# Routing, end and input of a four-layer fp32 model on one core, with 20 token slots as pairs of four k tiles by 512 columns

## The chip, the cores and the metric

One core of a Trainium2 chip (trn2). PE is TensorE (matmul), PEld its weight load, DVE VectorE, ACT ScalarE, POOL GpSimd, SP SyncE, which here only issues DMAs. All times are device microseconds of one execution of the whole program; the metric is the median of several executions, lower is better.

## The reference

Input x is 1 x 256 x 1024, all in float32. Two blocks of two layers each follow one another. Cut to what matters:

```python
# first block: an even layer, an odd layer, then rms_norm(x, final_norm)
def even_layer(x, g_norm, w_in, b_f, w_out):
    z = rms_norm(x, g_norm) @ w_in          # 8208 columns: qa ka va ga fa qb kb vb gb
    ya = forgetting_attention(qa, ka, va, log_sigmoid(fa + b_f))   # 16 heads of 64
    yb = dilated_attention(qb, kb, vb)                             # 16 heads of 64
    return x + concat([ya * silu(ga), yb * silu(gb)]) @ w_out
def odd_layer(x, g_norm, w_in, w_out):
    q, k, v, g = split(rms_norm(x, g_norm) @ w_in)     # 1024, 1024, 2048, 2048 columns
    y = head_group_norm(retention(rotate(q), rotate(k) / 16, v))   # 4 heads, v of 512
    return x + (y * silu(g)) @ w_out
# second block: layer_norm, then twice
    h = layer_norm(ALPHA * h + hybrid_mixer(h, ...))   # sparse attention and a short convolution
    h = layer_norm(ALPHA * h + f)                      # f: swiglu (l = 0), then
def moe_swiglu(h, w_router, wg, wu, wd):               # f of l = 1: 8 experts, 2 of them per token
    top_v, top_i = top_k(h @ w_router, 2)
    gate = sum(one_hot(top_i) * softmax(top_v))
    return sum(gate[e] * (silu(h @ wg[e]) * (h @ wu[e])) @ wd[e] for e in range(8))
```

## The kernel before

The 256 tokens are two tiles (NT, t = 0, 1) of 128; the model width is eight k tiles (KD). Weights come as **slots** of 128 x 2048 float32 (1 MB), 275 in all. For each slot SP issues a load into a raw buffer (L437; two raw buffers before the experts, four in them), ACT copies it rounded to fp32r into `w_hi` (`split_hi`, L1197), DVE writes the remainder to `w_lo` (`split_lo`, L1520), and PE multiplies each pair of operands in three matmuls: high with high, high with low, low with high (`parts_mm`, L566 to L568). The activations are split the same way (`x_hi`, `x_lo`; `y_hi`, `y_lo`; `t_hi`, `t_lo` at the routing). `w_hi`/`w_lo` are rings of four before the experts and three in them; `ahead(s)` on ACT and DVE splits slot s + 4 (or s + 3) once slot s is through. Each engine's instructions run in the order written; semaphores order them across engines: `lo_done` (slot ready), `used` (slot multiplied), `g_free` (one of three result banks `g_ps` free), `n_h`, `n_tr`, `n_hi`, `n_lo` (halves of a norm's rows, transposes and splits).

A **token slot** (`token_slot`) holds all eight k tiles for 256 output columns: per token tile eight k steps, each with a 128 x 128 block of x as the stationary operand and 256 weight columns moving, 48 matmuls in all. `rows_slot` has the weights stationary and 256 tokens moving, also 48. Output slots (`out_slot`) and expert slots have four k tiles and 512 columns, and so 24 and 12 matmuls of 512.

Order of the work. *Start:* norm 0 of both token tiles with `begin(0, ...)`: x is normalized on DVE (`summed`, `ready`, `finish`; POOL computes the inverse root as a power, `root`, DVE refines it, `newton`), transposed by PE, split, and multiplied with slots 0 and 1 as it comes. Slots 0 to 3 are the first v; then `narrow_product` (16 columns: forget gates) and slots 4 to 11. *Even layer:* two attentions of eight pairs of heads; PE runs one slot in each step (`among`): slots 12 to 23 and the gates 24 to 31, the second v being 20 to 23. *Retention:* v slots 40 to 47, q and k 48 to 55, gates 56 to 63. In the head loop PE does scores of head h, a gate slot (`G_AFTER`), and the head's output once DVE has the decayed scores (`decayed`, L1928, semaphore `r_dec`) and the norm of the head before (`r_norm`, L1954). ACT applies Silu to the gate slot, DVE multiplies (`gate_slot`, L1936, `r_y`). *Routing* (after slot 142, norm 5): per token tile the product with the router (`narrow_part`, 8 columns, 24 matmuls); the top two (`router`, L1701 to L1733, small DVE operations, each after the last); the ranks by two small matmuls; one-hot selections (`select`, L1743); `gather` (32 matmuls, L571) makes the transposed rows of the first two experts. `keep_busy` issues matmuls that nobody reads. The number of rounds is computed at L1731 to L1733, and `m_loops` releases it: SP waits for it before the load of slot 147 (`sp.wait_ge(m_loops, 1)`). *Experts:* four rounds of 33 slots, two experts each: `gate_up` (22), `down` (11), results scattered back by matmuls (`scatter`) at the end. *End:* the last scatter, two sums per token tile (L2182, L1567), norm 6 and two output DMAs (L462).

## Time and profile before

| | |
|---|---|
| median of 3 runs | 1439.88 us (1438.84 to 1441.04) |
| profiled execution | 1441.42 us, span 1439.6 us |
| PE, DVE, ACT, POOL busy | 96%, 68%, 53%, 7% |
| DMA | 305.84 MB, 212 GB/s over the span |
| chain that ended last | PE 75%, DVE 11%, DMA 4%, issue 4%, ACT 4% |

The span is the time from the first to the last instruction. Busy shares are averages over stages with different limits; the chain is followed back from the last instruction, so its shares tell which engine the end depended on. A matmul's recorded duration overlaps the next one's: the pace is the distance between starts.

### The profile page before, as it was taken

The page shows a single profiled execution, that of the slowest core. Times are in us where ns is not written, and L with a number is a line of the kernel's source. Part 1 is how long each engine was busy: PE and PEld are TensorE (multiplying, and loading weights), DVE is VectorE, ACT ScalarE, POOL GpSimd, SP SyncE. Part 2 cuts the span into 40 slices and gives each one's busy share as a digit, 9 for nine tenths or more (in the row PEclk, how much of TensorE's full clock was granted, in tenths as well). Part 3 has the DMA queues.
Part 4 walks back from the last instruction along what each step waited for, and adds up shares of the span by engine and source line. Part 5 has one row for each costly group of instructions (what it writes and reads, how often), then busy time and mean ns, then how long its engine had stood idle before and what let it go on. Part 6 is the DMA issues. An engine that isn't in the chain of part 4 may idle for free.

```text
span 1439.6 us, 22664 instructions
## 1 busy us (share of the span) xinstructions
PE 1384.1 (96%) x9117; PEld 1229.2 (85%) x9117; DVE 978.5 (68%) x1354; ACT 759.1 (53%) x915; POOL 101.6 (7%) x112
## 2 busy tenths in 40 slices
PE   5999999999999999999999999999999999999995
PEld 5999998789988889888999889887888888888883
DVE  5445656564766476867544476858788898898887
ACT  3445468425333327743443336742677677677672
POOL 1000013100001210001222010002000000000000
PEclk9999999999999999999999999998999999999998
DMA  6543344436543635534555545540798988889985
GB/s 223 194 178 143 118 147 146 145 135 232 192 147 118 219 126 189 192 106 164 203 188 190 180 154 201 195 163 31 299 355 315 342 326 341 344 323 356 327 334 218
DMA packets 43674, 305.84 MB, mean 212 GB/s; under 512 B 4864, under 2 KB 5120, under 8 KB 7744
## 3 DMA queue, kind: packets, MB, share of 16 engines
q1 hardware_dynamic: 41328, 295.69, 55.7%
q0 software_dynamic: 2256, 8.88, 1.8%
q8 instruction: 64, 1.05, 0.3%
q14 instruction: 26, 0.21, 0.0%
HBM read 303.51 MB, written 1.05 MB: 212 GB/s over the span
## 4 chain that ended last, share of the span: by engine, by line
PE 75%; DVE 11%; DMA 4%; issue 4%; ACT 4%; POOL 1%; DVEq 0%; SPq 0%; POOLq 0%; ACTq 0%
PE g_ps L566 18%; PE g_ps L568 17%; PE g_ps L567 17%; PE a_ps L566 4%; DMA raw<-w_dram 4%; PE a_ps L568 4%; PE a_ps L567 4%; PE a_ps L571 4%; DVE w_lo L1520 3%; ACT w_hi L1197 3%; PE a_ps L575 2%; PE o_ps L571 2%; DVE tiny L1567 1%; DVE x L1651 1%; POOL tiny L481 1%
## 5 line engine op out<-in xcount | busy, mean ns | idle before, releaser
L1520 DVE TENSOR_TENSOR w_lo<-raw,w_hi 128x2048 fp32r<-128x2048 f32 x240 | 548.6, 2291 | 233.3 <-ACT w_hi L1197 230.5
L1197 ACT ACTIVATE w_hi<-raw 128x2048 fp32r<-128x2048 f32 x240 | 459.7, 1915 | 245.4 <-PE a_ps L568 91.1
L566 PE MATMUL g_ps<-w_hi,x_hi 128*128 128x256 f32 (+1 forms) x720 | 244.8, 340 | 12.5 <-DVE x_lo L1617 8.5
L566 PE MATMUL g_ps<-x_hi,w_hi 128*128 128x256 f32 x880 | 252.6, 287 | 0.0
L567 PE MATMUL g_ps<-x_lo,w_hi 128*128 128x256 f32 x880 | 249.9, 284 | 0.0
L568 PE MATMUL g_ps<-x_hi,w_lo 128*128 128x256 f32 x880 | 249.8, 284 | 0.0
L568 PE MATMUL g_ps<-w_hi,x_lo 128*128 128x256 f32 (+1 forms) x720 | 239.3, 332 | 0.0
L567 PE MATMUL g_ps<-w_lo,x_hi 128*128 128x256 f32 (+1 forms) x720 | 239.0, 332 | 0.0
L566 PEld LDWEIGHTS g_ps<-x_hi,w_hi 128*128 128x128 f32 x880 | 169.8, 193 | 4.0 <-issue 3.9
L567 PEld LDWEIGHTS g_ps<-x_lo,w_hi 128*128 128x128 f32 x880 | 169.8, 193 | 0.0
L568 PEld LDWEIGHTS g_ps<-x_hi,w_lo 128*128 128x128 f32 x880 | 169.7, 193 | 0.0
L566 PEld LDWEIGHTS g_ps<-w_hi,x_hi 128*128 128x128 f32 x720 | 137.8, 191 | 29.4 <-DVE w_lo L1520 10.6
L566 PE MATMUL a_ps<-w_hi,y_hi 128*128 128x512 f32 x384 | 151.8, 395 | 3.9 <-DVE w_lo L1520 1.9
L568 PE MATMUL a_ps<-w_hi,y_lo 128*128 128x512 f32 x384 | 149.8, 390 | 0.0
L567 PE MATMUL a_ps<-w_lo,y_hi 128*128 128x512 f32 x384 | 149.7, 390 | 0.0
L568 PEld LDWEIGHTS g_ps<-w_hi,x_lo 128*128 128x128 f32 x720 | 137.8, 191 | 13.1
L567 PEld LDWEIGHTS g_ps<-w_lo,x_hi 128*128 128x128 f32 x720 | 138.1, 192 | 12.2 <-issue 0.2
L1520 DVE TENSOR_TENSOR w_in_raw<-raw,w_in_raw 128x2048 fp32r<-128x2048 f32 x35 | 80.2, 2291 | 54.9 <-ACT w_in_raw L1197 54.9
L566 PEld LDWEIGHTS a_ps<-w_hi,y_hi 128*128 128x128 f32 x384 | 72.1, 188 | 20.6 <-issue 4.5
L568 PEld LDWEIGHTS a_ps<-w_hi,y_lo 128*128 128x128 f32 x384 | 72.1, 188 | 15.4
L1197 ACT ACTIVATE w_in_raw<-raw 128x2048 fp32r<-128x2048 f32 x35 | 66.9, 1911 | 33.6 <-DMA raw<-w_dram 15.1
L567 PEld LDWEIGHTS a_ps<-w_lo,y_hi 128*128 128x128 f32 x384 | 72.2, 188 | 14.0
(287 smaller groups left out, 1996.7 us busy)
## 6 DMA issues: line engine op xcount, KB each, us to landing
raw<-w_dram SPq DMA_DIRECT2D x279, 1024.0 KB, 4.9
arena<-rows_dram POOLq DMA_DIRECT2D x3, 1024.0 KB, 5.4
x<-x_dram SPq DMA_DIRECT2D x2, 512.0 KB, 6.8
extra<-extra_dram POOLq DMA_DIRECT2D x1, 1024.0 KB, 5.6
extra<-rows_dram POOLq DMA_DIRECT2D x2, 512.0 KB, 3.7
y_spare<-rows_dram POOLq DMA_DIRECT2D x4, 256.0 KB, 4.8
out_dram<-x SPq DMA_DIRECT2D x2, 512.0 KB, 2.7
extra<-gains_dram SPq DMA_DIRECT2D x1, 512.0 KB, 4.5
```

The lines of the kernel that those rows point to most:

```text
L481: pool.tensor_tensor(tiny[:, 228 + t0:228 + t0 + n], tiny[:, 224 + t0:224 + t0 + n], tiny[:, 226 + t0:226 + t0 + n], ALU.pow).then_inc(roo ...
L566: pe.matmul(ps, lh, rh, start=start, stop=False, skip_group_check=True)
L567: pe.matmul(ps, lh, rl, start=False, stop=False, skip_group_check=True)
L568: return pe.matmul(ps, ll, rh, start=False, stop=stop, skip_group_check=True)
L571: return pe.matmul(ps, lhs, rhs, start=start, stop=stop, skip_group_check=True)
L575: return pe.transpose(ps, src, ident)
L1197: act.activation(w_hi[w_place(s)][:, :], raw[PLACE[s]][:, :], ACT.Copy).then_inc(hi_done, 1)
L1520: dve.tensor_tensor(w_lo[w_place(s)][:, :], raw[PLACE[s]][:, :], w_hi[w_place(s)][:, :].bitcast(F32), ALU.subtract).then_inc(lo_done, 1)
L1567: own(dve.bn_stats(tiny[:, 200 + 12 * t + 6 * b:206 + 12 * t + 6 * b], xs))
L1651: own(dve.scalar_tensor_tensor(xs, xs, scale, out_bank(t, b)[:, :], ALU.mult, ALU.add))
```

## The change

The layout of the weights, their number and bytes stay as they are; 20 slots hold other elements.

- **Input.** The host passes x also transposed, `xT`, and the first norm's gain as eight columns. Slots 0 to 3 are multiplied with the unnormalized `xT` times gain, split into `y_hi`, `y_lo` (`plain_slot`), and the copies of their results are scaled by the token's inverse root. PE starts with nine matmuls that nobody reads. The inverse roots are broadcast by two transposes, DVE scales `xT` from that bank, and one split makes `x_hi`, `x_lo` for slot 4 on. Order and queue position of the first DMAs change; `small` and `extra` are issued later by POOL.
- **Wide slots.** The second even v (20 to 23), retention's v (40 to 47) and gates (56 to 63) become pairs: a slot holds four k tiles and 512 columns, its pair the other four; two result banks (one per token tile) stay open over both, and are copied after the second. The decay of head h + 1 moves ahead of the moments of head h.
- **Routing.** The router product is made like the second block's gates: high and low part side by side as 48 stationary columns (`small_rows`), copied by ACT, added by `fold_rows`. POOL makes only the first `t_lo`, after norm 5, and DVE the second. The splits of slots 144 and 145, the counts (`round_counts`) and the memset of the accumulator move behind the selection. The fillers go from 16 + 14 + 4 to 3 + 12 + 8. Slot 143 needs only half of x_lo.
- **End.** The first expert's half of the last scatter goes ahead of the last two slots, which are multiplied by column halves. The sums come with the additions, the variance from ACT (Square with accumulation), and four output DMAs replace two.

The core of the diff (indentation cut by eight):

```diff
-    load_x(0)
-    sp.dma_start(extra[:, G_AT:G_AT + D], a["gains"][0]).then_inc(gain_in, 16)
-    sp.dma_start(const[:, 0:P], a["const"][:, 0:P]).then_inc(ident_in, 16)
+    sp.dma_start(const[:, 0:C_CAUSAL], a["const"][:, 0:C_CAUSAL]).then_inc(ident_in, 16)
+    for b in range(2):
+        sp.dma_start(xT[:, 4 * b:4 * b + 4, :], a["xT"][:, 4 * b:4 * b + 4, :]).then_inc(xT_in[b], 16)
     load(0, 0)
-    load_x(1)
     load(1, 1)
-    sp.dma_start(const[:, P:N_CONST], a["const"][:, P:N_CONST]).then_inc(const_in, 16)
+    for t in range(NT):
+        load_x(t)
+    sp.dma_start(const[:, C_CAUSAL:N_CONST], a["const"][:, C_CAUSAL:N_CONST]).then_inc(const_in, 16)
     sp.dma_start(vec[:, :], a["vec"]).then_inc(vec_in, 16)
     for s in range(2, MOE + PLACES):
         load(s, s)
...
+        for b in range(2):
+            cols = slice(512 * b, 512 * b + 512)
+            sp.wait_ge(n_h, 4 * 6 + 2 * t + b + 1)
+            sp.dma_start(out.rearrange("b (t p) d -> p (b t) d", p=P)[:, t, cols], x[:, t, cols]).then_inc(out_done, 16)
+    sp.wait_ge(out_done, 64)
...
+    pool.dma_start(small_raw, a["small"].rearrange("p k (a b) -> p k a b", a=3)).then_inc(small_in, 16)
     pool.wait_ge(n_h, 4)
-    pool.dma_start(extra[:, G_AT:G_AT + D], a["gains"][1]).then_inc(odd_gain_in, 16)
+    pool.dma_start(extra[:, 0:E_ALL], a["extra"][0][:, 0:E_ALL]).then_inc(extra_in, 16)
+    pool.wait_ge(n_lo, 4)
+    pool.dma_start(extra[:, G_AT:G_AT + D], a["gains"][0]).then_inc(odd_gain_in, 16)
...
             for t in range(NT):
-                pool.wait_ge(m_thi, t + 1)
-                pool.tensor_tensor(t_lo[:, t, :], x[:, t, :], t_hi[:, t, :].bitcast(F32),
-                                   ALU.subtract).then_inc(m_tlo, 1)
-            load_both_rows(6)
-            two_roots()
+                a_ = tiny[:, 224 + t:225 + t]
+                pool.wait_ge(e_var, t + 1)
+                own(pool.tensor_tensor(a_, end_var[:, t:t + 1], end_eps, ALU.add))
+                own.sync()
...
+    def wide_mm(s, half, t, ks):
+        w = weights(s + half, (4, 512))
+        for k in ks:
+            mm = parts_mm(g_ps[bank_of(s + t)][:, :], pick(from_x, lambda u: u[:, k, t * P:(t + 1) * P]),
+                          pick(w, lambda u: u[:, k - 4 * half, :]), k == 0, k == KD - 1)
+        return mm
...
+    def wide_slot(s, half):
+        pe.wait_ge(lo_done, s + half + 1)
+        for t in range(NT):
+            if half == 0:
+                wide_free(s, t)
+            mm = wide_mm(s, half, t, range(4 * half, 4 * half + 4))
+        mm.then_inc(used, 1)
...
+    def small_rows(i, seg):
...
         def part_of(t, ks):
             for k in ks:
                 parts_come(i, t, k)
                 to = slice(t * P, (t + 1) * P)
...
+                pe.matmul(a_ps[0][0:48, to], small[:, k, seg, :, :].rearrange("p a b -> p (a b)"), x_hi[:, k, to],
...
-                mm = pe.matmul(a_ps[0][0:24, to], small[:, k, 1 + l, 0, :], x_lo[:, k, to],
+                mm = pe.matmul(a_ps[0][0:24, to], small[:, k, seg, 0, :], x_lo[:, k, to],
...
+    def plain_slot(s):
+        w = weights(s, (KD, S))
+        if s > 0:
+            pe.wait_ge(lo_done, s + 1)
+        if g_nth[s] > 0:
+            pe.wait_ge(g_free[bank_of(s)], g_nth[s])
+        for half in range(2):
+            if s == 0 and half == 0:
+                pe.wait_ge(half_lo, 1)
+            elif s == 0:
+                pe.wait_ge(lo_done, 1)
+            for t in range(NT):
+                for k in range(4 * half, 4 * half + 4):
+                    if s == 0 and t == 0:
+                        pe.wait_ge(u_lo, k + 1)
+                    mm = parts_mm(g_ps[bank_of(s)][:, t * S:(t + 1) * S],
+                                  pick(from_y, lambda u: u[:, k, t * P:(t + 1) * P]),
+                                  pick(w, lambda u: u[:, k, :]), k == 0 and t == 0, k == KD - 1)
+        mm.then_inc(used, 1)
+    pe.wait_ge(u_hi, 4)
+    early = y_hi[:, 0:2, :].rearrange("p a b -> p (a b)")
+    for _ in range(9):
+        pe.matmul(g_ps[2][:, :], early[:, 0:P], early[:, :], start=True, stop=True, skip_group_check=True)
+    for s in range(2):
+        plain_slot(s)
     pe.wait_ge(ident_in, 16)
-    begin(0, token_part(0, 0), token_part(0, 1))
+    pe.wait_ge(n_h, 4)
+    for t in range(NT):
+        tr = turned(a_ps[0][:, t * P:(t + 1) * P], tiny[:, 228 + t:229 + t].to_broadcast([P, P]))
+    tr.then_inc(n_tr, 4)
     for s in range(2, 4):
-        even_slot(s)
+        plain_slot(s)
+    pe.wait_ge(n_lo, 4)
     pe.wait_ge(small_done, 1)
     narrow_product(0, HF)
...
-    keep_busy(16, 2, G_ALL)
+    keep_busy(3, 2, G_ALL)
+    fold_rows(DEPTH)
+    keep_busy(12, 2, G_ALL)
...
-    keep_busy(14, 2, G_ALL)
+    keep_busy(8, 2, G_ALL)
...
-    keep_busy(4, 2, G_ALL)
...
-        pe.wait_ge(m_xlo, 4 + 4 * i)
+        pe.wait_ge(m_xlo, (4 if earlier else 2) + 4 * i)
...
+                    pe.wait_ge(m_xlo, 4)
                 if u == 5:
...
+            return
+        pe.wait_ge(m_hid, UNITS + UNITS * i)
+        pe.wait_ge(m_osb, 2 + 4 * i)
+        for t in range(NT):
+            for n in range(2):
+                scatter(banks[t][n], t, n, 0, True, False)
+        for n in range(2):
+            for c in (UNITS - 2, UNITS - 1):
+                pe.wait_ge(lo_done, MOE + FT + c + 1 + 33 * i)
+                for k in range(2):
+                    mm = half_of(c, k, n)
+                if n == 1:
+                    mm.then_inc(used, 1)
+                elif c == UNITS - 1:
+                    mm.then_inc(m_first, 1)
...
+    act.wait_ge(ident_in, 16)
+    for k in range(KD):
+        act.wait_ge(xT_in[k // 4], 16)
+        act.activation(y_hi[:, k, :], xT[:, k, :], ACT.Copy, scale=norm_col[:, k:k + 1]).then_inc(u_hi, 1)
+    act.wait_ge(raw_in[0], 16)
+    act.activation(w_hi[0][:, 0:SLOT // 2], raw[0][:, 0:SLOT // 2], ACT.Copy).then_inc(half_hi, 1)
+    act.activation(w_hi[0][:, SLOT // 2:], raw[0][:, SLOT // 2:], ACT.Copy).then_inc(hi_done, 1)
+    for s in range(1, RING_BEFORE):
+        split_hi(s, 0, s)
+    act.wait_ge(n_h, 4)
+    even_slot(0)
+    for b in range(2):
+        act.wait_ge(zT_made, 4 * b + 4)
+        act.activation(x_hi[:, 4 * b:4 * b + 4, :], xT[:, 4 * b:4 * b + 4, :], ACT.Copy).then_inc(n_hi, 2)
+    act.wait_ge(small_in, 16)
+    act.activation(small_hi, small_raw, ACT.Copy).then_inc(small_hi_done, 1)
...
-        s = OD_G + u
-        act.wait_ge(used, s + 1)
-        if u >= 3:
-            act.wait_ge(r_y, u - 2)
-        act.activation(gate_view(s), g_ps[bank_of(s)][:, :], ACT.Silu).then_inc(g_free[bank_of(s)], 1)
-        ahead(s)
+        act.wait_ge(used, OD_G + u + 1)
+        for e in ((u - 1, u) if u % 2 else ()):
+            s = OD_G + e
+            if e >= 3:
+                act.wait_ge(r_y, e - 2)
+            act.activation(gate_view(s), g_ps[bank_of(s)][:, :], ACT.Silu).then_inc(g_free[bank_of(s)], 1)
+        ahead(OD_G + u)
...
-            ahead(L_WO[l] + 2 + t)
+            if not (l and t):
+                ahead(L_WO[l] + 2 + t)
             if l:
                 act.wait_ge(n_h, 4 * i + 2 * t + 2)
                 act.activation(t_hi[:, t, :], x[:, t, :], ACT.Copy).then_inc(m_thi, 1)
+        if l:
+            act.wait_ge(narrow_full, 2 + DEPTH)
+            act.activation(rows24, a_ps[0][0:48, 0:S], ACT.Copy).then_inc(rows_copied, 1)
+            ahead(L_WO[l] + 3)
...
+                if not last:
+                    act.wait_ge(used, MOE + FT + (6 if e == 0 else 11) + 33 * i)
                 act.wait_ge(m_back, 1 + i)
                 for n in range(2):
...
+                act.wait_ge(e_mean, t + 1)
+                act.activation(unread[:, t, :], x[:, t, :], ACT.Square, bias=end_bias[:, t:t + 1], scale=D ** -0.5,
+                               accum_out=end_var[:, t:t + 1]).then_inc(e_var, 1)
...
-        rest_of_norm(i, lambda: tile(0), lambda: tile(1), (last, last + 1))
+        rest_of_norm(i, lambda: tile(0), lambda: tile(1), () if i == 5 else (last, last + 1))
...
+        dve.wait_ge(rows_folded, 1 + DEPTH)
+        chain(lambda: dve.tensor_copy(lg, a_ps[1][:, 0:64].rearrange("p (a b) -> p a b", a=2)[:, :, HF:HF + NE]))
         best(on1, mx[0])
         chain(lambda: dve.scalar_tensor_tensor(lg, on1, NEG, lg, ALU.mult, ALU.add))
...
-    dve.wait_ge(gain_in, 16)
+    dve.wait_ge(ident_in, 16)
+    for k in range(KD):
+        dve.wait_ge(u_hi, k + 1)
+        dve.scalar_tensor_tensor(y_lo[:, k, :], xT[:, k, :], norm_col[:, k:k + 1], y_hi[:, k, :].bitcast(F32),
+                                 ALU.mult, ALU.subtract).then_inc(u_lo, 1)
+    halves = slice(0, SLOT // 2), slice(SLOT // 2, SLOT)
+    for half, made, done in zip(halves, (half_hi, hi_done), (half_lo, lo_done)):
+        dve.wait_ge(made, 1)
+        dve.tensor_tensor(w_lo[0][:, half], raw[0][:, half], w_hi[0][:, half].bitcast(F32), ALU.subtract).then_inc(done, 1)
+    split_lo(1, 0, 1)
     for t in range(NT):
         dve.wait_ge(x_in[t], 16)
         for b in range(2):
             summed(0, t, b)
         ready(0, t)
-        finish(0, t)
-        split_lo(t, 0, t)
-        low_part(0, t)
+    for t in range(NT):
+        dve.wait_ge(root_done, asked[t])
+        newton(tiny[:, 224 + t:225 + t], tiny[:, 228 + t:229 + t], tiny[:, 230 + t:231 + t])
+    dve.tensor_copy(tiny[:, 240:242], tiny[:, 228:230]).then_inc(n_h, 4)
+    split_lo(2, 0, 2)
+    dve.wait_ge(n_tr, 4)
+    for k in range(KD):
+        dve.scalar_tensor_tensor(xT[:, k, :], xT[:, k, :], norm_col[:, k:k + 1], a_ps[0][:, 0:S],
+                                 ALU.mult, ALU.mult).then_inc(zT_made, 1)
+    split_lo(3, 0, 3)
...
-        dst = rv[:, :, u * S:(u + 1) * S]
-        dve.tensor_tensor(dst, dst, gate_view(s).rearrange("p (a b) -> p a b", a=2), ALU.mult).then_inc(r_y, 1)
+        dst = rv[:, u % 2, u // 2 * RV:(u // 2 + 1) * RV]
+        dve.tensor_tensor(dst, dst, gate_view(s), ALU.mult).then_inc(r_y, 1)
...
     gated = 0
+    decayed(0)
     for h in range(RH):
-        decayed(h)
         for u in G_AFTER[h]:
             ahead(OD_G + u)
-            while gated <= u and gated < 2 * h:
+            while (gated | 1) <= u and gated < 2 * h:
                 gate_slot(gated)
                 gated += 1
+        if h < RH - 1:
+            decayed(h + 1)
         dve.wait_ge(r_out, h + 1)
...
+        ahead(L_WO[1] + 2)
...
+        ahead(L_WO[1] + 3)
+        round_counts()
+        dve.memset(f_acc[:, :, :], 0.0).then_inc(m_acc, 1)
...
+            own(dve.tensor_tensor_reduce(xs, xs, banks[t][n][:, :], 1.0, 0.0, ALU.add, ALU.add, end_sum[:, t, n:n + 1]))
+        def mean_of(t):
             own.sync()
-            summed(6, t, n)
-        dve.wait_ge(m_sct, 2 * before + 1)
+            dve.tensor_scalar(end_bias[:, t:t + 1], end_sum[:, t, 0:1], end_sum[:, t, 1:2], -D ** -1.5,
...
+        def scattered(n):
+            dve.wait_ge(m_sct, 2 * before + 1 + n)
+            own(dve.tensor_tensor(tiny[:, 238 + n:239 + n], const[:, 0:1], const[:, 1:2], ALU.add))
...
-        gathered(0, 1)
-        ready(6, 0)
-        centre(6, 0)
-        finish(6, 0)
...
+        scattered(1)
+        for t in range(NT):
+            gathered(t, 1)
+            mean_of(t)
+        for t in range(NT):
+            y = tiny[:, 228 + t:229 + t]
+            own.sync()
+            own(dve.scalar_tensor_tensor(z[:, t, :], x[:, t, :], end_mean[:, t:t + 1], gain_of(6), ALU.add, ALU.mult))
+            roots.append(0)
+            dve.wait_ge(root_done, len(roots))
+            newton(tiny[:, 224 + t:225 + t], y, tiny[:, 230 + t:231 + t])
+            for b in range(2):
+                dve.scalar_tensor_tensor(x[:, t, cols(b)], z[:, t, cols(b)], y, bias_of(6, b), ALU.mult, ALU.add).then_inc(n_h, 1)
...
+def wide_slots(w):
+    n = w.shape[1] // 512
+    return w.reshape(2, 4, P, n, 512).transpose(3, 0, 2, 1, 4).reshape(2 * n, P, SLOT)
```

## Rows read from the trace of the kernel before

**Rows 1.** page: busy time of each engine; granted clock in 40 slices

```profile
PE 1384.1 (96%) x9117; PEld 1229.2 (85%) x9117; DVE 978.5 (68%) x1354; ACT 759.1 (53%) x915; POOL 101.6 (7%) x112
...
PEclk9999999999999999999999999998999999999998
```

**Rows 2.** waits of PE: who waited for whom, total us, times, longest

```profile
PE a_ps L575 <- DVE arena L1604: 9.5, 1, 9.5
```

**Rows 3.** timeline of PE (start us, us): 256 columns, then 512

```profile
255.81 0.28 PE L567 MATMUL g_ps<-x_lo,w_in_raw 128*128 128x256 f32 x1
...
258.45 0.28 PE L568 MATMUL g_ps<-x_hi,w_in_raw 128*128 128x256 f32 x1
...
800.15 0.39 PE L566 MATMUL a_ps<-w_in_raw,y_hi 128*128 128x512 f32 x1
...
804.68 0.39 PE L568 MATMUL a_ps<-w_in_raw,y_lo 128*128 128x512 f32 x1
```

**Rows 4.** chain of waits to 32 us (start, us), then timeline rows

```profile
2.13 9.08 DMA raw<-w_dram
...
13.18 2.29 DVE w_lo L1520
...
45.77 0.17 PE L566 MATMUL a_ps<-small,x_hi 128*128 128x16 f32 x1
...
405.56 0.43 DVE L1919 TENSOR_TENSOR arena<-part 128x256 f32<-128x256 f32 x1
```

**Rows 5.** windows: busy us per engine, PEclk, DMA share, GB/s

```profile
23.00:25.60 2.60, 2.54 (x12) 2.54 (x12) 0.00 (x1) 0.00 (x0) 0.00 (x0) 0.50 0.81 265
...
409.90:477.30 67.40, 64.90 (x442) 56.90 (x442) 41.59 (x66) 22.12 (x22) 9.86 (x10) 1.00 0.37 132
993.10:998.40 5.30, 5.24 (x25) 5.24 (x25) 5.10 (x4) 2.88 (x3) 2.34 (x1) 0.50 0.00 0
```

**Rows 6.** chain of waits in retention, start and us

```profile
426.88 4.15 PE a_ps L571 x14
...
447.88 2.41 PE a_ps L571 x5
```

**Rows 7.** routing: DVE timeline, chain row, PE timeline

```profile
985.89 3.44 DVE L1594 SCALAR_TENSOR_TENSOR x<-x,tiny,extra 128x1024 f32<-128x1024 f32 x1
...
998.89 1.72 DVE L1702 TENSOR_TENSOR tiny<-tiny 128x16 f32<-128x16 f32 x1
...
1004.61 1.76 DVE L1723 MEMSET arena<- 128x2048 f32 x1 [0.38 <-issue]
...
1008.57 4.11 PE a_ps L571 x32
...
534.79 0.22 PE L706 MATMUL a_ps<-x_hi,small 128*48 128x128 f32 x1
...
535.69 0.22 PE L708 MATMUL a_ps<-x_lo,small 128*24 128x128 f32 x1
```

**Rows 8.** PE at slot 147, page's loads, chain, window of a round

```profile
1025.23 0.48 PE L566 MATMUL g_ps<-w_hi,x_hi 128*128 128x512 f32 x1
...
raw<-w_dram SPq DMA_DIRECT2D x279, 1024.0 KB, 4.9
...
1108.78 8.66 DMA raw<-w_dram
...
1084.10:1187.50 103.40, 102.67 (x503) 85.38 (x502) 90.09 (x73) 74.01 (x65) 0.00 (x0) 1.00 0.89 336
```

**Rows 9.** the end: chain row, DVE, POOL, and SP's output transfers

```profile
1420.17 1.40 PE g_ps L571 x6
...
1427.38 1.28 DVE L1594 SCALAR_TENSOR_TENSOR x<-x,tiny,arena 128x1024 f32<-128x1024 f32 x1
...
1427.56 1.53 POOL L481 TENSOR_TENSOR tiny<-tiny 128x1 f32<-128x1 f32 x1 [426.28 <-DVE tiny L1584]
...
1431.14 5.73 SPq L462 DMA_DIRECT2D out_dram<-x  x2
```

180 lines of the change are left out of this document (104 added, 76 removed).

## The prediction

> **What bounds the kernel now.** I read the page first. PE is busy 96% of the span and its granted clock is full in nearly every slice [rows 1], so a gain has to come from fewer PE columns or loads, from stretches where PE runs at the low clock, or from the gaps. The waits of PE itself are short in sum; the largest single one is the first transpose, 9.5 us [rows 2]. The steady stretches are paced by PE alone. In one, 22 intervals of a 256-column matmul take 2.64 us (0.120 us each, 48 to a slot: 5.76 us); in another, 20 intervals with 512 columns take 4.53 us (0.2265 us each, 24 to a slot: 5.44 us) [rows 3]. The chain of waits leaves PE in four places that this change touches: the first 28 us, the four heads of retention, the routing at 985 to 1014 us, and the end after 1420 us.
>
> **The start.** Today PE waits for the load issued at 2.13 that lands at 11.21, its split on ACT (1.92) and DVE (2.29), and the split of the normalized x; then, half-way, for a second norm and split. Slot 3 ends as the narrow product begins, at 45.77 us [rows 4]. It also works 23.0 to 25.6 us at half clock [rows 5].
> After the change no PE work before slot 4 needs the norm. The DMA order becomes constants (68 KB), transposed x (1 MB), slot 0, slot 1, x. That is 732 KB less ahead of slot 0 than today; 2,848 KB landed in the 9.08 us to 11.21, so its share is 2.3 us and slot 0 lands at about 8.9 (estimate). Half a slot on ACT is half of 1.92 plus latency, 1.05, and on DVE 1.2: PE starts at 11.25. The scaled splits of x (8 on ACT of about 0.35, 8 on DVE of about 0.43, the 128x256 row of [rows 4]) lie under the load of slot 0, and the nine warm-up matmuls (512 columns at half clock, twice 0.2265, 4.1 us from about 6.1) too. From there four slots of 5.76 and two small transposes (0.4) follow: 11.25 + 23.04 + 0.4 = 34.7.
> What could be late is checked by chaining the rows. Slot 1: lands 11.5, ACT to 13.4, DVE to 15.9, wanted at 17.0. DVE then does the sums of squares (4 of about 0.65), the two roots' newton steps (0.6 each) and posts the root at 20.4; slot 2's low part ends at 22.7 and PE wants it at 23.3. The eight scalings of the transposed x out of PSUM take 8 x 0.40 = 3.3, and slot 3's low part ends at 28.8, wanted at 29.0. The ACT queue has a new long wait: it scales slot 0's output and then stands on the load of slot 4 (issued at 22.7, landed 27.5) before it makes x_hi; behind it x_hi and x_lo end at 32.9 and the small weights at 34.2, just before PE asks. **Gain 45.8 - 34.7 = 11.1**, with 9 to 13 as ends: a cold first slot costs 1.3 (14 matmuls at 0.21 instead of 0.12 [rows 4, 5]), a scaling of 0.69 instead of 0.40 each costs 2.1, and and a first load as much earlier again as the estimate above says gives 2.
>
> **Wide slots.** 20 slots go from 5.76 to 5.44 us: 0.32 each. The four of the second v: 1.28, less 0.3 because both banks of the last pair are now copied (2 x 0.6 on ACT) before the scores may start: **1.0**. The eight v slots of retention run back to back, the copy of a pair needs banks that PE wants 2.7 us later: **2.6**. Of the eight gate slots four lie inside the head loop, where PE does not set the pace alone. There the chain goes from the end of a gate slot through Silu, ACT's split, DVE's split 2.29, moments, root, the two scalings, and decay, to the next outputs: from 416.95 to 426.88, and a similar one, with the gate products, ends at 447.88 [rows 6]. Moving the decay ahead of the moments shifts 0.55 us within that chain and saves nothing; two Silus before a split instead of one add 0.5 us to every second chain. By that arithmetic the loop ends 0.4 later after its first slot than now. Outside it two slots give 0.32 each ahead of the loop, slot 62 gives 0.32, and slot 63 with the wait for y_lo 1.15 (DVE has no gate product ahead of the casts there), less 0.3 for the last turned outputs, which wait for both last gate products. **1.4**, between 0.4 and 2.6.
>
> **Routing.** Four things leave the path. POOL's t_lo runs beside DVE's centring of x, which takes 3.44 us instead of 1.28: 2.15. The second t_lo holds a 16-column operation for 1.72 instead of 0.17: 1.55. The 24 narrow matmuls per token tile at half clock (0.21 each, 5.3 us in all) become 16 of 128 columns (0.90 us from first to last at full clock, about 1.8 at half): 3.3 off, but a copy on ACT, three filler matmuls and the fold come back, 1.8. The memset of 1.76 and four count steps of 0.17 to 0.2 go behind the gather: 2.2 [rows 5, 7]. DVE's t_lo (1.2) waits for ACT's t_hi and ends before the fold. PE has 15 fillers before the ranks where it had 16; the last 12, part at half clock, take about 4.2 us and end at 998.8, later than m_on at 997.4. Chained, the gather starts at 1001.35 instead of 1008.57: 7.2. Two split instructions also move: slot 144's low part now precedes x_lo, slot 145's and the counts follow.
> Not all of this reaches the slots, since the counts release SP's loads. Today SP has loads 147 to 149 issued at 1008.56, long before their use. After the change the last x_lo ends at 1006.8, split 145 at 1009.1, the counts at 9.8, SP issues at 10.8 and the first load lands 4.9 later; ACT 1.92 and DVE 2.29 follow. Slot 147 starts at 1019.9 instead of 1025.2 [rows 8]. **5.3**; 8.2 if the load were there in time, 4 if a queued load's 8.66 [rows 8] came in between. The rounds behind are paced by PE (33 slots in about 102.7 of the 103.4 us of the window [rows 8]), so the shift stays.
>
> **End.** The first half of the scatter (1.86) goes ahead of the last two slots, and these are done column half by half, so that ACT, DVE and the last scatter of the first half are hidden. PE ends its last slot at 1421.2 instead of 1420.17. The sums come with the additions (0.69 each) and four bn_stats of 0.69 go: 2.8. Variance goes to ACT (1.2 plus its read) and an addition to POOL. Today POOL's power of a number takes 1.53 beside the 1.28 us centring, ending 0.42 after it [rows 9]; the new one has two POOL steps behind the same cover. Chained: gathered from 22.85, centring 26.75 to 28.03, root 29.1, second tile to 34.45, last output DMA 34.5 instead of 36.54, and 256 KB land 0.4 faster than 512: **2.4**, between 1 and 4.
> The Trainium skill weighs on one step here: "SBUF — State Buffer", section "Who interferes with whom", says that a DVE instruction with two SBUF inputs and a GpSimd instruction that reads SBUF shut each other out, the first one holding the ports, while a DVE instruction with one SBUF input isn't touched. The 3.44 and 1.53 us rows agree with its first half; no row has POOL's t_lo beside DVE's x_lo, which reads PSUM and SBUF and will now run together. By the rule that costs nothing; were it wrong, the routing would give 1.2 less.
>
> **Sum.** 11.1 + 1.0 + 2.6 + 1.4 + 5.3 + 2.4 = 23.8. The profiled execution took 1441.42 (span 1439.6), so 1417.6 in it; its time is 1.5 above the median, 1439.88, from which I forecast 1416.1. The smallest terms give 9 + 0.4 + 2.0 + 0.5 + 4 + 1 = 17 (1423), the largest 13 + 1.3 + 2.6 + 2.6 + 8.2 + 4 = 32 (1408).
>
> **Rivals.**
> - *PE stays cold.* There are 23 fillers in the routing where there were 34, and PE idles about 1 us before its first slot. For it: 993.1 to 998.4 us is at half clock today although fillers run on both sides. Against: retention, with its gaps of up to 1 us, is at full clock; the half clock at 23.0 follows a longer wait, for the second norm [rows 5]. Price: 1.3 at the start, the gather's 4.11 [rows 7] doubled at most. Time 1421. The Trainium skill, "TensorE: Matmul & The Clock Gate", section "HAM oscillation — how this bites in real kernels", tells of kernels re-throttled by each wait for a DMA, which is this rival.
> - *Loads are early.* The loads land as PE wants them in the routing, and the first MB at 400 GB/s: 2.9 + 2 more. Time 1411.
> - *Slower: the ring of loads sets the experts' pace.* Released late, each load may stay queued behind two others. Four places, each load + 1.92 + 2.29: with 4.9 us it is 9.1 for four slots, with the queued 8.66 it is 12.9, against PE's 12.4 (4 x 3.11) [rows 8]. It decides from a landing of 8.2 us; if every one took 9.5, 132 slots would be 0.31 longer each, 42 us, and 1457 us in all. Against: a load issued as DMA is idle can catch up, and DMA is only 0.89 busy.
> - *The wide pairs stall.* If both banks of a pair must be free at once, the 5.0 of these slots vanish: 1420.5.
>
> **Numbers.** Forecast as summed 0.70 (own range 1412 to 1420), cold PE 0.11, early loads 0.11, wide pairs 0.05, ring 0.03. Range 1409.5 to 1422. Differences under about 0.2% can't be told from none. Faster by more than that 0.96, within 0.01, slower 0.03.
>
> **What would show it.** The narrow product begins near 34.7 us, and slots 20 to 23, 40 to 47 end 5.44 apart outside attention. The head loop keeps DVE in its chain. L1594's successor at the routing takes 1.28. ACT waits for the DMA at the fifth expert slot. The last output DMA is issued about 14.3 us after PE's last weight slot started its scatter half, 2 us sooner than now. A start that begins over 13 us, or a first expert round longer than 103 us, would make the forecast wrong.

## The result

The changed kernel takes 1426.7 us (median of 4 runs, 1421.7 to 1427.0), the kernel before 1440.4 (4 runs): a ratio of 0.990, with an interval of 0.9875 to 0.992. It is faster by 13.7 us, 1.0%; 23.8 were forecast, and 1416.1 us with a range of 1409.5 to 1422. The profiled execution went from a span of 1439.6 to 1424.7, 14.9 less.

The page of the changed kernel, busy times and granted clock (as [rows 1]):

```profile
PE 1370.3 (96%) x8609; PEld 1192.3 (84%) x8609; DVE 977.2 (69%) x1369; ACT 763.7 (54%) x923; POOL 94.8 (7%) x114
...
PEclk9899999999999999999999999999999999999998
...
raw<-w_dram SPq DMA_DIRECT2D x279, 1024.0 KB, 4.9
```

Its waits of PE (who waited for whom, total us, times, longest), as [rows 2]:

```profile
PE g_ps L903 <- ACT y_hi L1378: 8.4, 1, 8.4
PE g_ps L585 <- DVE w_lo L1650: 4.8, 6, 2.6
...
PE a_ps L590 <- DVE arena L2110: 3.2, 2, 2.1
...
PE g_ps L585 <- ACT arena L1428: 2.5, 1, 2.5
PE a_ps L585 <- DVE small L2000: 1.4, 1, 1.4
```

PE lost 13.8 us of work and the 9.5 us wait for the first norm. In its place stand five smaller waits, in the order of the list: warm-up matmuls that wait for x, the weights of single slots, head products that wait for VectorE's scaling, a bank, and the small weights of the narrow product. Each of the last three has an experiment below.

The whole course is read best from the ends of the weight slots: the last matmul of each slot in the trace. The table gives the end of slot 3, then how long each stretch of slots took, and from slot 272 to the end of the span (us). Only stretches that differ are shown. x5_half_after and x6_half_before leave out a part of the computation.

```
kernel            slot 3    3-4   19-23   39-47   55-64  142-145 145-147  147-272  272-end
before             45.9    14.2    27.3    50.1    73.2    41.0     5.7    385.6    25.8
before, again      46.3    14.2    27.3    50.1    73.2    41.0     5.7    384.8    25.8
changed            35.8    17.5    26.2    50.3    72.8    29.8     9.2    389.7    22.1
x0_after (same)    36.3    15.4    26.2    50.3    74.5    31.1     9.1    388.5    22.3
x1_start           36.7    12.6    26.2    52.0    72.9    29.8    10.8    386.1    22.3
x2_copies          36.8    15.4    26.2    47.4    74.5    29.8    10.7    384.7    22.8
x3_counts          36.3    15.1    26.2    50.4    74.5    31.4     6.6    386.5    22.2
x7_heads           36.2    17.3    26.2    50.4    71.9    31.1     9.0    386.5    22.4
x8_four            37.0    12.6    26.2    47.4    71.9    30.1     6.6    386.4    22.8
x9_table           35.4    14.2    26.2    47.5    72.0    30.1     6.6    384.8    22.9
u1_tokens          36.4    15.5    26.2    50.1    74.5    31.1     9.1    384.0    23.1
u2_late_scatter    35.8    16.8    26.2    51.8    74.5    29.8    10.6    384.2    24.1
x5_half_after      36.1    15.3    26.2    50.3    74.6    31.1     9.1    381.7    21.8
x6_half_before     44.5    14.2    27.3    50.1    73.2    41.0     5.7    382.2    25.0
```

The kernels named x, u and b are the experiments below. A part of what differs between them is no order of work but TensorE's granted clock, which in some traces fell to 0.50 behind a wait and in others not. The traces of the changed order show it in five places. At the start it fell to 0.50 between 39 and 42 us in all of them, and stayed there longest in those with 16.8 to 17.5 in their 3-4 column. At slot 42 it fell in x1_start and u2_late_scatter, which have 52.0 and 51.8 for slots 39 to 47. In the head loop it fell in the six with 74.5 or 74.6; in slots 142 to 145 in the five with 31.1 to 31.4; and at slot 147 in the three with 10.6 to 10.8. Each fall at the last four places costs 1.3 to 1.7 us.

Terms of the forecast against the two profiled executions, before less changed:

| stretch | forecast | measured |
|---|---|---|
| start, to the end of slot 4 | 11.1 | 6.85 |
| second even values, to slot 39 | 1.0 | 0.7 |
| retention values | 2.6 | -0.15 |
| gates, head loop, to slot 142 | 1.4 | 0.3 |
| routing, slots 142 to 147 | 5.3 | 7.65 |
| experts, 147 to 272 | 0 | -4.1 |
| end, from slot 272 | 2.4 | 3.7 |
| sum | 23.8 | 14.9 |

### The profile page after: what moved, and what is told of

Its sections match the earlier page's. It is cut to its first block, busy times and chain, and to the rows that moved or that the text cites. A ratio compares the mean times of both kernels' runs of the same rounds, so it can differ in the third digit from the quotient of the medians.

```text
span 1424.7 us, 21674 instructions
## 1 busy us (share of the span) xinstructions
PE 1370.3 (96%) x8609; PEld 1192.3 (84%) x8609; DVE 977.2 (69%) x1369; ACT 763.7 (54%) x923; POOL 94.8 (7%) x114
## 4 chain that ended last, share of the span: by engine, by line
PE 68%; DVE 12%; DMA 8%; ACT 5%; issue 5%; POOL 1%; DVEq 0%; SPq 0%; ACTq 0%
PE g_ps L585 16%; PE g_ps L587 15%; PE g_ps L586 15%; DMA raw<-w_dram 8%; DVE w_lo L1650 5%; PE a_ps L590 4%; PE a_ps L585 4%; PE a_ps L587 4%; PE a_ps L586 4%; ACT w_hi L1288 4%; PE a_ps L594 2%; PE o_ps L590 2%; DVE x L1781 1%; DVE tiny L1697 1%; POOL tiny L493 1%
## 5 line engine op out<-in xcount | busy, mean ns | idle before, releaser
L585 PE MATMUL g_ps<-w_hi,x_hi 128*128 128x512 f32 (+1 forms) x552 | 208.8, 378 | 11.1 <-DVE w_lo L1650 4.8
L587 PE MATMUL g_ps<-w_hi,x_lo 128*128 128x512 f32 (+1 forms) x552 | 203.5, 369 | 0.0
L586 PE MATMUL g_ps<-w_lo,x_hi 128*128 128x512 f32 (+1 forms) x552 | 203.3, 368 | 0.0
L585 PEld LDWEIGHTS g_ps<-w_hi,x_hi 128*128 128x128 f32 x552 | 104.0, 188 | 32.7 <-DVE w_lo L1650 7.8
L587 PEld LDWEIGHTS g_ps<-w_hi,x_lo 128*128 128x128 f32 x552 | 104.0, 188 | 18.1
L586 PEld LDWEIGHTS g_ps<-w_lo,x_hi 128*128 128x128 f32 x552 | 104.2, 189 | 16.1 <-issue 0.2
L585 PEld LDWEIGHTS a_ps<-w_hi,y_hi 128*128 128x128 f32 x384 | 72.1, 188 | 20.5 <-issue 2.9
L1288 ACT ACTIVATE w_in_raw<-raw 128x2048 fp32r<-128x2048 f32 x35 | 66.9, 1910 | 35.1 <-DMA raw<-w_dram 16.8
```

Of the source, the lines that this page charges most:

```text
L585: pe.matmul(ps, lh, rh, start=start, stop=False, skip_group_check=True)
L586: pe.matmul(ps, lh, rl, start=False, stop=False, skip_group_check=True)
L587: return pe.matmul(ps, ll, rh, start=False, stop=stop, skip_group_check=True)
L1288: act.activation(w_hi[w_place(s)][:, :], raw[PLACE[s]][:, :], ACT.Copy).then_inc(hi_done, 1)
```

## Experiments

**The same kernels again.** Other runs of both, to see what repeats.

> The changed kernel once more, unchanged. Its profiled run lost 2.9 us at slots 173 to 212 that three other versions, whose experts are the same, didn't lose (21.4 us from slot 172 to 179 as in the kernel before, instead of 23.4). Theory: this loss is a chance of the single run, in the supply of the loads, and no price of the change: here the stretch takes 21.4 us, and the median is about 1423 to 1425 us. Rival: it belongs to the changed kernel, whose expert slots start at another time than in the others: 23.4 us again, and about 1426.7.

> The kernel before once more, unchanged, for a second trace of it. Slots 147 to 274 took 391.9 us in its first trace, and 393.0 to 397.2 us in six traces of versions of the changed kernel. Theory: the changed kernel's experts lose 1 to 5 us more for want of loads, since PE reaches them sooner: here 391 to 392.5 us again. Rival: the stretch varies from run to run by as much in both kernels, and the first trace of before was a lucky one: 394 us or more.

Measured: the changed kernel 1426.9 us (1423.5 to 1428.1), so the rival held. The kernel before gave 1440.7, and 384.8 us for slots 147 to 272 (391.2 to slot 274), so the theory held for it. Still, the versions below with full loads, whose experts are the same, took 384.0 to 386.5. Two things differ between traces of one program: the clock (above), and this stretch.

**Conversions at the start** (ScalarE). The second argument leaves out the split at the end of even_slot.

```diff
-            even_slot(0)
+            even_slot(0, False)
...
             act.activation(small_hi, small_raw, ACT.Copy).then_inc(small_hi_done, 1)
+            ahead(0)
```

> The changed kernel with one thing moved on ScalarE: the conversions of z and of the small weights stand ahead of the split of slot 4, which in the trace of the changed kernel waited for its load until 30.56 us and held them back. Theory: the 4 us that the start fell short of come from here. The narrow product then begins with the end of slot 3 at 35.8 us instead of 37.21 (1.4 us), and as TensorE no longer idles ahead of it, the clock should fall later than at 39.7 us, which gives up to 1.6 us more: slot 4 ends 1.4 to 3.0 us sooner, and the end as much sooner. Rival: what is late is the low part on VectorE (its queue holds the split of slot 3 until 29.7 us) or the gate of the clock, and the product takes longer by what it begins sooner: slot 4 ends within 0.5 us of before.

Measured: 1423.0 us (1418.9 to 1428.3), ratio 0.989 (0.987 to 0.9905). The ratios of the single orders, this and the next ones, can't be told from the changed kernel's 0.990 (0.9875 to 0.992), so that each is judged by its own stretch. Slot 4 comes 12.6 us after slot 3, against 15.1 to 17.5 in the eight traces with the old order there, and ends at 49.3 us against 51.4 to 53.5. ScalarE in the changed kernel, then PE in both (start us, us, then what it waited for):

```profile
30.56 1.92 ACT L1288 ACTIVATE w_hi<-raw 128x2048 fp32r<-128x2048 f32 x1 [6.85 <-DMA raw<-w_dram]
32.38 1.99 ACT L1388 ACTIVATE x_hi<-arena 128x1024 fp32r<-128x1024 f32 x2
...
37.21 0.25 PE L585 MATMUL a_ps<-small,x_hi 128*128 128x16 f32 x1 [1.42 <-DVE small L2000]
```

```profile
36.48 0.17 PE L585 MATMUL a_ps<-small,x_hi 128*128 128x16 f32 x1
```

Windows of both (busy us by engine, PEclk, DMA share, GB/s), the changed kernel first:

```profile
39.00:41.00 2.00, 2.00 (x15) 2.00 (x14) 2.00 (x2) 0.00 (x0) 0.00 (x0) 0.67 0.37 84
41.00:43.00 2.00, 2.00 (x11) 2.00 (x11) 0.47 (x1) 0.00 (x0) 0.00 (x0) 0.50 0.97 401
43.00:45.40 2.40, 2.40 (x12) 2.40 (x13) 0.00 (x0) 1.28 (x1) 0.00 (x0) 0.50 0.98 358
```

```profile
39.00:41.00 2.00, 2.00 (x21) 2.00 (x20) 0.59 (x1) 0.00 (x0) 0.00 (x0) 1.00 0.83 324
41.00:43.00 2.00, 2.00 (x13) 2.00 (x13) 0.00 (x0) 1.59 (x1) 0.00 (x0) 0.62 0.84 352
```

The 1.4 us wait is gone and the clock falls later, so that 21 matmuls instead of 15 run between 39 and 41 us. The theory held: slot 4 ends 4.0 us sooner than in the changed kernel's first trace, 2.4 sooner than in x0_after. A part of that is the clock, which was at 0.50 for a shorter time. At slot 42 this version lost 1.7 (52.0 instead of 50.3). The wait there is the one of the next experiment and no longer than in the changed kernel (2.6 us against 2.5); behind it the clock fell:

```profile
318.00:320.00 2.00, 2.00 (x7) 1.53 (x6) 1.51 (x2) 0.82 (x1) 0.00 (x0) 0.50 0.28 33
```

**Copies of a pair of banks** (ScalarE).

```diff
                 if m % 2:
...
-                ahead(OD_V + m)
+                    ahead(OD_V + m - 1)
+                    ahead(OD_V + m)
```

> The changed kernel with ScalarE's order in the retention values changed: the copies of a pair of banks stand ahead of the two splits of weights, the first of which waited for its load until 318.00 us. Theory: the 2.5 us that TensorE stood between 317.93 and 320.45 are the wait for a bank of the first pair, whose copies were queued behind that split; they go, slot 47 ends about 2.5 us sooner, and the end too. Rival: TensorE waits there for weights or for the low part, or the splits that now come later run late: slot 47 ends within 0.5 us of the changed kernel's 350.66, or later.

Measured: 1421.4 us (1421.2 to 1424.4), ratio 0.988 (0.986 to 0.989); slots 39 to 47 in 47.4 us. The changed kernel, PE and ScalarE:

```profile
320.45 0.50 PE L585 MATMUL g_ps<-w_hi,x_hi 128*128 128x512 f32 x1 [2.52 <-ACT arena L1428]
...
318.00 1.91 ACT L1288 ACTIVATE w_hi<-raw 128x2048 fp32r<-128x2048 f32 x1 [5.82 <-DMA raw<-w_dram]
319.81 1.07 ACT L1428 ACTIVATE arena<-g_ps 128x512 f32<-128x512 f32 x2
```

With the copies first:

```profile
314.20 1.09 ACT L1428 ACTIVATE arena<-g_ps 128x512 f32<-128x512 f32 x2 [3.07 <-PE g_ps L587]
317.01 1.92 ACT L1288 ACTIVATE w_hi<-raw 128x2048 fp32r<-128x2048 f32 x1 [1.72 <-DMA raw<-w_dram]
```

The bank was full because its copy stood behind a split that stood behind a DMA. The theory held: with the copies moved, PE has no wait there and slot 42 takes 5.44 us instead of 8.25.

**Retention values as token slots again.** Packing, matmuls and copies of slots 40 to 47 as before the change.

> The changed kernel with the eight slots of the retention values as token slots with 256 columns again, as before the change. By the forecast the wide form was worth 2.6 us. By the trace it brought 0.32 us for each slot, 2.5, and lost 2.5 in the one wait for a bank at slot 42, so that undoing it costs nothing: slot 47 ends within 0.6 us of the changed kernel's, counted from the end of slot 39 (50.2 us), and the median is the same within 1 us. Rival, the forecast's size was right and the wait at slot 42 would have come anyway (its load is late): 2 us slower.

Measured: 50.1 us for slots 39 to 47 against 50.3, and 1423.7 us (1421.2 to 1425.4), ratio 0.987 (0.986 to 0.989). To slot 142 it is level with x0_after (974.1 and 973.8 us), as the theory says: eight wide slots were worth nothing as built, 2.7 with x2_copies (50.1 to 47.4). That it ended below x0_after lies wholly in slots 147 to 272 (384.0 us instead of 388.5), which this edit doesn't touch.

**Order of VectorE in the head loop.**

```diff
             for h in range(RH):
-                for u in G_AFTER[h]:
-                    ahead(OD_G + u)
...
+                if h == 0:
+                    ahead(OD_G + 1)
+                dve.wait_ge(r_out, h + 1)
+                moments(lambda t: [a_ps[1 + t][:, :]], EPS)
                 if h < RH - 1:
                     decayed(h + 1)
-                dve.wait_ge(r_out, h + 1)
-                moments(lambda t: [a_ps[1 + t][:, :]], EPS)
                 y = inverse_root()
...
                 ins.then_inc(r_norm, 1)
+                if h < RH - 1:
+                    u = h + 2
+                    ahead(OD_G + u)
...
```

The edit does less than the expectation says. The split and the gate products of the next slot move from the top of one turn of the loop to the end of the turn before, which is the same place in VectorE's queue: they still stand ahead of the next head's statistics. What moves is the decay of the next head, from ahead of the statistics to behind them.

> The changed kernel with VectorE's order in the head loop of the retention changed: the statistics and scaling of a head's outputs stand ahead of the split of weights and the products with the gates. In the trace of the changed kernel TensorE waited for them 1.2 us at the second head (until 419.48 us) and 2.1 us at the fourth (until 440.74), in three other traces with a clock of 0.50 for some 4 us behind the second wait, which cost 1.7 us more. Theory: the gain of the wide gate slots ended there; the waits go, slot 61 ends 3 us sooner, up to 5 where the clock fell too. Rival: the splits that now come later are late for TensorE, or their loads are: under 1 us.

Measured: 1423.8 us (1423.6 to 1425.3), ratio 0.988 (0.986 to 0.989). Slots 55 to 64 take 71.9 us; the changed kernel takes 72.8 in one trace and 74.5 in the other. Waits of PE in the loop, with the order changed:

```profile
PE a_ps L590 <- DVE arena L2107: 2.3, 2, 1.6
```

Only 0.9 of the 3.2 us went, about 0.5 at each of the two waits, which is the decay of 0.55. VectorE ahead of the second of these waits, in the changed kernel and then here (L2090 the gate product, L2082 the decay, L1770 the statistics):

```profile
432.03 2.29 DVE L1650 TENSOR_TENSOR w_in_raw<-raw,w_in_raw 128x2048 fp32r<-128x2048 f32 x1 [3.08 <-ACT w_in_raw L1288]
434.24 1.28 DVE L2090 TENSOR_TENSOR arena<-arena,prob 128x512 f32<-128x512 f32 x2
435.44 0.55 DVE L2082 TENSOR_TENSOR prob<-a_ps,extra 128x384 f32<-128x384 f32 x1
435.91 1.28 DVE L1770 BATCH_NORM_STATS2 tiny<-a_ps 128x6 f32<-128x512 f32 x2
```

```profile
434.17 1.29 DVE L2090 TENSOR_TENSOR arena<-arena,prob 128x512 f32<-128x512 f32 x2
435.37 1.29 DVE L1770 BATCH_NORM_STATS2 tiny<-a_ps 128x6 f32<-128x512 f32 x2
```

The third head's outputs are done on PE at 431.7 us in both, but the statistics begin at 435.9 and 435.4: the split, which waited for ScalarE, and the gate product stand ahead of them. From there to the end of the scaling it is 4.7 us. An order that really puts the statistics ahead of the split wasn't run, so what the whole wait is worth stays open. The other gain is the clock. In x2_copies, with the old order, PE waited 2.05 us and then ran at 0.50:

```profile
436.88 4.51 PE L590 MATMUL a_ps<-arena,prob 128*128 128x512 f32 x6 [2.05 <-DVE arena L2111]
...
438.00:440.00 2.00, 2.00 (x3) 0.67 (x2) 1.18 (x1) 0.00 (x0) 0.00 (x0) 0.50 0.00 0
```

and with the new order the same six took 2.81:

```profile
440.20 2.81 PE L590 MATMUL a_ps<-arena,prob 128*128 128x512 f32 x6 [1.58 <-DVE arena L2107]
```

So 0.9 us of the gain is the order's and 1.7 the clock's: 2.6 against x0_after, where the clock had fallen. It fell in none of the three traces with the new order (waits of at most 1.6 us) and in six of the eight with the old one (2.1 us). The expected 3 us didn't come, and the theory was not tested as worded.

**Count of the rounds earlier** (VectorE). The memset now stands behind the experts' first split.

```diff
                 select(slice(0, 2), 0)
+                round_counts()
                 ahead(L_WO[1] + 2)
...
-                round_counts()
-                dve.memset(f_acc[:, :, :], 0.0).then_inc(m_acc, 1)
```

> The changed kernel with the number of rounds worked out right behind the selection matrices (four instructions of 0.15 us) instead of behind two splits of weights, and the memset of the accumulator behind the first split of the experts. The loads of slots 147 to 149 then are issued at about 992.7 to 997 us instead of 1000.70. Theory A, the experts lost their 5 us for want of a lead of the loads: slot 147 starts at about 1007 instead of 1009.84, the lead of the splits before TensorE is 3 us or more instead of 1.2, and of the 5 us lost in the four rounds at least 2 come back: end 4.5 to 7 us sooner. Theory B, the loads run at what the queues can move and no lead helps beyond the first round: slot 147 3 us sooner and the end 3 us sooner or less.

Measured: 1423.5 us (1421.8 to 1424.4), ratio 0.989 (0.987 to 0.990). First load of the experts, changed kernel and this one, and PE's wait in the changed kernel:

```profile
1000.70 3.61 SPq L447 DMA_DIRECT2D raw<-w_dram  x4
...
1009.84 0.50 PE L585 MATMUL g_ps<-w_hi,x_hi 128*128 128x512 f32 x1 [2.59 <-DVE w_lo L1650]
```

```profile
993.80 10.17 SPq L447 DMA_DIRECT2D raw<-w_dram  x4
```

Slots 142 to 147 took 38.0 us instead of 40.2 (x0_after, with the same clock in them): 2.2, less than the 3 expected. Theory A fell: slots 147 to 272 took 386.5 us, as in versions with late counts. The lead of 1.2 us that it took for too short was a misreading too: in slots 150 to 271 a slot's low part ends 1.4 us ahead of PE (median) in the kernel before as in the changed one.

**Half of each load.**

```diff
-  sp.dma_start(raw[..][:, :], a["w"][s])
+  cols = slice(0, SLOT // 2) if to >= MOE + 8 else slice(0, SLOT)
+  sp.dma_start(raw[..][:, cols], a["w"][s][:, cols])
```

> The changed kernel, but from the ninth expert slot on only half of each slot's weights is loaded (columns 0 to 1023), so that part of the computation is left out; all other instructions stay. Theory A and B, the loads cost the experts their time: the losses against the kernel before at slots 173, 177, 199, 245, 265 and 269 to 273 go, the end comes 5 to 8 us sooner than the changed kernel's 1424.7. Rival C, the splits on ScalarE and VectorE or the order of their queues cost it: the end stays within 1 us.

> The kernel before, but from the ninth expert slot on only half of each slot's weights is loaded, so that part of the computation is left out. In the changed kernel this shortened slots 147 to 274 from 397.2 to 388.9 us. Theory A, the kernel before had no lack of loads, the changed one has, as its loads begin late: here the stretch shrinks by under 2 us from 391.9. Theory B, at the round's ends the loads are what sets the pace in both kernels: here too about 388.9, 3 us less, and the end 3 us or more sooner than 1440.

Measured: 1420.1 us (1418.9 to 1421.6) and 1435.8 (1435.1 to 1436.6). Slots 147 to 272 in windows, for the kernel before, the changed kernel, and the changed kernel with half loads:

```profile
1028.30:1413.80 385.50, 382.72 (x1874) 318.72 (x1872) 336.68 (x264) 277.94 (x245) 0.00 (x0) 1.00 0.90 338
```

```profile
1012.90:1402.60 389.70, 384.74 (x1875) 318.55 (x1875) 336.37 (x264) 277.44 (x245) 0.00 (x0) 1.00 0.90 335
```

```profile
1013.60:1395.30 381.70, 381.70 (x1876) 319.35 (x1875) 337.83 (x265) 278.47 (x245) 0.00 (x0) 1.00 0.53 172
```

With half loads PE hardly stands: the longest wait in that stretch is 0.5 us in one of the two kernels, and there is none in the other. So full loads cost the kernel before 2.7 to 3.4 us (385.6 and 384.8 less 382.2) and the changed one 2.3 to 8.0 (384.0 to 389.7 less 381.7); rival C fell, and B's "in both" held. What makes one run lose 8 us and the next 2 stays open: the losses lie at the downward slots of the rounds (23.4 and 23.9 us for slots 172 to 179 in the changed kernel, 20.5 to 22.9 in the rest with full loads), and they don't follow the lead or the counts. The two traces of the unaltered changed kernel are the two slowest of ten in this stretch; by chance alone that comes once in 45 times, which is too little to say that the program is prone to it or that it was unlucky twice.

**The scatter behind the last slots.**

> The changed kernel with the scatter of the first half of the experts' outputs put back behind the last two weight slots. The forecast counted it (1.86 us) as taken off the path, with slots 273 and 274 ending 1.0 us later. Theory: the last slot ends 1.9 us sooner, the first sum of VectorE begins 0 to 0.5 us later, since the last conversions on ScalarE and VectorE hide most of the scatter: the end 0.5 us later than now at most. Rival: all of it lies on the path: 1.5 to 1.9 us later, counted from slot 272.

The edit puts the four first-half scatters of the last round behind both column halves. Measured: 1429.8 us (1426.7 to 1434.2), ratio 0.993 (0.991 to 0.994), and 24.1 us from slot 272 to the end. The changed kernel has 22.1 and 22.3 there, the other versions with its end and full loads 22.1 to 23.1, so that the cost is 1.0 to 2.0 us and the rival's 1.5 to 1.9 is the better of the two. From the end of slot 274 alone it is 1.2 us more (15.8 instead of 14.5 in all the others). The median is 6 us above u1_tokens' on the same chip; the traced execution is the fastest of the four, and what the rest is made of is not shown. Waits of PE there, without and with the early scatter (x0_after):

```profile
PE a_ps L585 <- DVE w_lo L1650: 2.2, 2, 1.5
```

```profile
PE g_ps L590 <- DVE o_lo L2329: 0.7, 1, 0.7
PE a_ps L585 <- DVE w_lo L1650: 0.3, 1, 0.3
```

The scatter costs next to nothing where the change put it, as PE would stand there for the last low parts: slots 273 and 274 took 8.3 us without it and 7.5 to 8.5 with it.

**All four orders, and the table load.**

> All four orders at once: conversions at the start, copies of the pair, counts of the rounds, statistics of the heads. Theory: the four waits lie in series on TensorE's path, so that their gains add: about 2.7 for the start, 2.5 for the copies, 3.2 for the heads and 2 to 3 for the counts, 10 to 11 us below the changed kernel on this chip, some 1413 us. Rival: the loads of the experts set the pace and take half of it back: 1417 to 1420 us.

> The four orders of the last comparison, and a one-element copy on ScalarE ahead of its first wait, so that the table load of 1.28 us, which in the changed kernel began as the transposed x landed (5.30 us), is done by then. Theory: the conversions of x begin at 5.3 instead of 6.59, the split of slot 0 follows with its landing, at about 8.7 to 9.0 instead of 9.80, and all behind it is about 1 us sooner: some 1413 us. Rival: the first load lands no sooner than 9.8: no gain, 1414.

Measured: x8_four 1414.0 us (1412.5 to 1418.4), ratio 0.9815 (0.980 to 0.983), 13.0 below x0_after on the same chip. The four add, as far as stretches of two traces can tell: 2.8 from slot 3 to slot 4 (0.7 of it had been lost ahead of slot 3), 2.9 for the copies, 2.6 in the head loop (1.7 of it clock), 3.5 from slot 142 to 147 (1.0 of it clock); 2.1 more in slots 147 to 272 can be chance, and the end took 0.5 longer. It beats both kernels. x9_table gave 1415.7 (1412.7 to 1417.1), ratio 0.982 (0.980 to 0.983), no gain. ScalarE in it:

```profile
0.73 1.28 ACT L1378 ACT_TABLE_LOAD   x1 [0.73 <-PEq L2486]
...
5.37 3.30 ACT L1382 ACTIVATE y_hi<-arena,const 128x256 fp32r<-128x256 f32 x8 [3.13 <-DMA arena<-xT_dram]
9.49 1.06 ACT L1384 ACTIVATE w_hi<-raw 128x1024 fp32r<-128x1024 f32 x1 [0.83 <-DMA raw<-w_dram]
```

The table load is hidden, x is converted 1.2 us sooner, and ScalarE then waits for slot 0, whose load lands at 9.49. Of 9.80 only 0.3 was the table's, so the rival's reason held. Slot 3 ends at 35.4 us, the earliest of all, and slot 4 at 49.6 as in x8_four, since the clock fell sooner after it (0.75 between 38 and 40 us, 0.50 to 44).

## Why the prediction was wrong

The sum came out 8.9 us short in the profiled execution (14.9 instead of 23.8). The steps that failed are the queue and the clock at the start (4.2), the pace of the experts (4.1), the bank in the retention values (2.7), the head loop (1.1) and the second even values (0.3); that the routing and the end gave 3.7 more than forecast hides a part of it.

**Start: 6.85 instead of 11.1.** "Slot 0 lands at about 8.9" was 0.6 early (9.5 in nearly every trace) and the table load cost 0.3 more, so that PE starts at 12.36 instead of 11.25 (the last 0.2 lie between the two half conversions and PE) and slot 3 ends at 35.8 instead of 34.7. Then "issued at 22.7, landed 27.5": the load of slot 4 was issued at 22.97 and landed at 30.56, 7.6 us instead of the 4.8 I took:

```profile
22.97 7.57 DMA raw<-w_dram
```

It took 7.0 to 7.9 in all eleven traces of the changed order, against about 4.8 for most others. POOL's transfers of the small weights and tables landed at 23.6 and 25.6 us and so ran beside its beginning; that they are the cause is not shown. The conversions behind it made the narrow product 1.4 late. The chain had named this queue and found it "just before PE asks", a margin of 0.5 us on an unqueued load. Last, the narrow product was not priced at a clock: from about 40 us it ran at half (windows above) and took 8.0 us (37.21 to 45.19) where it had taken 6.2 (45.77 to 51.99), its last 2 us at half clock then too. This is *PE stays cold*, in a place where I didn't look. These three, 1.1, 1.4 and 1.8, are the 4.2 that are missing.

**Retention values: 0 instead of 2.6.** The pace of 5.44 is right (x2_copies 47.4 against 50.1). The rival *the wide pairs stall* came true for one pair, though not by its reason (both banks of a pair free at once): the step that failed is that I checked when PE wants a bank, not what stands ahead of the copy on ScalarE. The rival's own time was added up wrongly too, 1416.1 + 5.0 is 1421.1 and not 1420.5.

**Head loop: 0.3 instead of 1.4.** VectorE's chain sets the end, as said, but PE reached it sooner and waited (1.2 and 2.1 us), so that the gain ended there. "Moving the decay ahead of the moments ... saves nothing" was right and too kind: it costs 0.5 us at each of the two heads where PE waited, as x7_heads shows. "Retention, with its gaps of up to 1 us, is at full clock" held in the profiled run and in one other; behind the gap of 2 us that the change made, the clock fell in six traces, 1.7 us each, which turns this term negative there.

**Routing: 7.65 instead of 5.3, two errors of opposite sign.** The gather began 17.2 us sooner, 9.5 more than slot 142's end, against 7.2 in the forecast; and slot 143 starts on two of the four x_lo, which I hadn't priced: 142 to 145 is 11.2 shorter. The twelve fillers took 2.9 us at full clock, not 4.2: the half clock of the kernel before in its routing [rows 5] didn't come back in the profiled run, so that *PE stays cold* was wrong here in spite of fewer fillers. The late count then took 3.5 back (145 to 147: 9.2 instead of 5.7), more than the 1.9 forecast. Where the clock fell in the routing (0.61 between 982 and 986 us in x0_after) it cost 1.3. The centring, once 3.44 beside POOL's work [rows 7], no longer has it beside it and takes 1.28:

```profile
977.03 1.28 DVE L1747 TENSOR_TENSOR x_lo<-a_ps,x_hi 128x512 fp32r<-128x512 f32 x2
978.23 1.28 DVE L1724 SCALAR_TENSOR_TENSOR x<-x,tiny,extra 128x1024 f32<-128x1024 f32 x1
...
981.49 2.38 POOL L571 TENSOR_TENSOR y_lo<-x,y_hi 128x1024 fp32r<-128x1024 f32 x1 [3.74 <-DVE x L1737]
...
982.13 1.35 DVE L1747 TENSOR_TENSOR x_lo<-a_ps,x_hi 128x512 fp32r<-128x512 f32 x2 [0.72 <-ACT x_hi L1306]
```

The last two rows run together and x_lo is hardly slowed: the same two instructions without POOL's subtraction, in the first row, take 1.28 us, and 1.35 beside it. By the Trainium skill, "SBUF — State Buffer", section "Who interferes with whom", a DVE instruction with only one SBUF input isn't touched by GpSimd. The trace agrees within 0.07 us, and the 1.2 us set against it was not lost.

**Experts: -4.1 instead of 0.** "The rounds behind are paced by PE ..., so the shift stays" failed. Of the 0.7 us of idle time in the window of one round [rows 8], 0.6 was one wait for a low part, and half loads take such waits away: over four rounds the kernel before lost 3 us to its loads, the changed one 2 to 8. Why the profiled run lost 8 stays open. The *ring of loads* rival had the right resource, but not at 0.31 us a slot.

**End: 3.7 instead of 2.4.** Counted from the last slot, the first centring began 0.6 sooner than chained and the inverse root was ready 1.0 sooner, so that the last output DMA was issued 12.1 us behind it and not 13.3 (the 14.3 among the prediction's signs counts from the slot end of the kernel before). It landed after 2.05 us instead of 2.66, 0.2 more than forecast. The extra us for the last two slots came (1.2).
